# Expert blocks of two 64-row halves with own experts as column tiles, and a second accumulator

## The reference, cut to what matters

```python
def swiglu(x, w_in, w_out):
    g, up = jnp.split(x @ w_in, 2, axis=-1)
    return (jax.nn.silu(g) * up) @ w_out
...
    def body(acc, blk):
        tok, gw, e = blk
        yb = swiglu(xt[tok], w_exp_in[e], w_exp_out[e]) * gw[:, None].astype(xt.dtype)
        return acc.at[tok].add(yb), None
...
    u = ln_plain(x) * (1.0 + scale2) + shift2
    x = ln_affine(DN_ALPHA * x + gate2 * moe(u, p), p['ln2_g'], p['ln2_b'])
```

## Time and profile before

| | |
|---|---|
| median of 3 runs | 2882.27 us (2881.45 to 2883.31) |
| span of the profiled execution | 2881.8 us |
| PE busy | 2738.3 us (95%) |
| DVE / ACT / POOL busy | 1581.8 (55%) / 691.3 (24%) / 1076.2 us (37%) |
| expert loop on PE | 1450.85 us to about 2826 us |
| output stage | from 2829.66 us to the end |

### The profile page before, as it was taken

The page is one execution under the profiler, slowest core; times in us unless marked ns, Lnnn a source line. Parts: engine busy times, 40 slices in busy tenths (PEclk is TensorE's granted clock), DMA queues, the critical chain, the costliest instruction groups (busy, mean ns, idle before and its releaser), DMA issues.

```text
span 2881.8 us, 31407 instructions
## 1 busy us (share of the span) xinstructions
PE 2738.3 (95%) x9145; PEld 1334.1 (46%) x9145; DVE 1581.8 (55%) x2551; ACT 691.3 (24%) x1204; POOL 1076.2 (37%) x1128
## 2 busy tenths in 40 slices
PE   7999999899999999899899999999999999999992
PEld 2345444455555455455444444444444444444440
DVE  4477356778877577778733344334343343333336
ACT  2354354366666311111100000000000000000004
POOL 2002001100000123233456656566565666556654
PEclk9999999899999999999899999999999999999996
DMA  9531010310000311311288798986978688899847
GB/s 350 182 115 55 19 33 8 128 44 12 12 12 8 136 59 59 109 60 59 76 268 233 229 324 228 315 253 166 285 220 264 183 248 248 257 306 287 244 96 255
DMA packets 189138, 464.37 MB, mean 161 GB/s; under 512 B 22524, under 2 KB 47294, under 8 KB 187646
## 3 DMA queue, kind: packets, MB, share of 16 engines
q1 hardware_dynamic: 138142, 311.89, 30.3%
q0 software_dynamic: 50912, 151.41, 21.3%
HBM read 359.28 MB, written 99.75 MB: 159 GB/s over the span
## 4 chain that ended last, share of the span: by engine, by line
PE 58%; DVE 4%; DMA 2%; issue 1%; POOL 1%; ACT 0%; DVEq 0%; SPq 0%; POOLq 0%
PE mx_pH L1263 30%; PE mx_pU L1280 15%; PE mx_pA L1901 3%; PE mx_pL L1901 3%; PE mx_pU L1963 2%; PE mx_pH L1926 2%; PE mx_pB L1934 1%; DMA s_acc<-mx_wso,ex_sidx 1%; PE mx_pB L1250 1%; DVE ring L1397 1%; DMA kT<-s_u,ex_gidx 1%; PE mx_pA L1938 0%; PE mx_pU L1911 0%; DVE mx_st L1723 0%; DMA ring<-s_acc 0%
## 5 line engine op out<-in xcount | busy, mean ns | idle before, releaser
L1263 PE MATMUL mx_pH<-ring,mx_wsi 128*128 (+1 forms) x2080 | 937.2, 593 | 6.4 <-DVE mx_h L1181 3.4
L1096 POOL DMA_INDIRECT kT<-s_u,ex_gidx x516 | 570.4, 1105 | 158.9 <-issue 153.5
L1263 PEld LDWEIGHTS mx_pH<-ring,mx_wsi 128*128 128x128 f32 x2080 | 385.4, 190 | 443.7 <-issue 443.7
L1280 PE MATMUL mx_pU<-qT,mx_hT 128*128 x1040 | 467.6, 592 | 1.5 <-DVE mx_wso L1204 1.5
L1177 DVE STREAM_TRANSPOSE mx_wsi<-kT 128x1024 f32<-128x1024 f32 x130 | 161.6, 1243 | 350.4 <-DMA kT<-s_u,ex_gidx 350.3
L1280 PEld LDWEIGHTS mx_pU<-qT,mx_hT 128*128 128x128 f32 x1040 | 197.5, 190 | 250.0 <-issue 250.0
L1120 POOL DMA_INDIRECT s_acc<-mx_wso,ex_sidx x130 | 212.2, 1632 | 189.5 <-DVE mx_wso L1204 126.7
L1204 DVE SCALAR_TENSOR_TENSOR mx_wso<-mx_pU,mx_wsi 128x1024 f32<-128x1024 f32 x130 | 166.9, 1284 | 186.5 <-PE mx_pU L1280 182.7
L1151 ACT ACTIVATE mx_hT<-mx_pB 128x256 f32<-128x256 f32 x130 | 49.8, 383 | 868.3 <-PE mx_pB L1250 868.3
L639 PE MATMUL fr_pF<-fr_uT,fr_wf 128*128 128x512 f32 x512 | 224.9, 595 | 1.3 <-ACT fr_uT L333 1.3
L1181 DVE TENSOR_TENSOR mx_h<-mx_silu,mx_pH 128x256 f32<-128x256 f32 x130 | 54.1, 416 | 305.9 <-ACT mx_silu L1141 305.6
(11 more groups left out here) (317 smaller groups left out, 3166.6 us busy)
## 6 DMA issues: line engine op xcount, KB each, us to landing
ring<-in_w_exp_in SPq DMA_DIRECT2D x64, 2048.0 KB, 13.8
qT<-in_w_exp_out SPq DMA_DIRECT2D x64, 1024.0 KB, 16.3
fr_wq<-in_w_ada SPq DMA_DIRECT2D x32, 512.0 KB, 4.9
kT<-s_u,ex_gidx POOLq DMA_INDIRECT x520
fr_wf<-in_w_in SPq DMA_DIRECT2D x16, 512.0 KB, 5.7
s_u<-v SPq DMA_DIRECT2D x16, 512.0 KB, 2.6
ring<-s_acc SPq DMA_DIRECT2D x16, 512.0 KB, 13.1
y<-ring SPq DMA_DIRECT2D x16, 512.0 KB, 6.7
```

Source lines behind the costliest of these rows:

```text
L1096: nc.gpsimd.indirect_dma_start(xg[:, u, g, :], None, u2_q, bass.IndirectOffsetOnAxis(ap=gidx[:, u, g:g + 1].bitcast(U32), axis=0)).then_in ...
L1263: m = nc.tensor.matmul(pH[:], xT[:, u, k, :], wi[:, bass.ds(slot, 1), k, :].rearrange("p a f -> p (a f)"), start=(k == 0), stop=(k == KD - 1))
L1280: m = nc.tensor.matmul(pY[:, h, :], hT[:, c, :], wo[:, bass.ds(slot, 1), c, h * 512:(h + 1) * 512].rearrange("p a d -> p (a d)"), start=(c ...
```

## The change

A block keeps its 128 rows, but it is made of two halves of 64 rows (`HALVES`, `ROWS`), each of one expert; neighbouring halves can belong to different experts. An expert has ceil(count / 64) halves, at least one, the first expert at least two. The places of the lists, `s_block` and the running count are in halves; the running count that the weight ring uses is rounded up to blocks.

On PE each matmul of `first`, `second` and `gated` becomes two, with 64 stationary columns each: the lower half goes to PSUM partitions 0 to 63, the upper to 64 to 127 (column tiles). The lower half reads the weights from the ring. The upper half reads them from a place of its own, one copy of an expert's weights, which ACT fills for every block: three copies for the input weights once `first` of the block before is done, one for the output weights once `second` of the block before is done. ACT reads the expert's number with a register load of its own. The transposes of `gated` are now matmuls by the identity.

On SP the loads of input and output weights have semaphores of their own; in each turn SP asks for an input load, waits for the output load of the expert before, asks for the output load, and waits for the input load.

The two halves of a block can hold the same token, so the upper rows are added into a second accumulator, rows T + P on of `s_acc`. It is cleared during the attention by 17 transfers of 512 KB. In `output` each tile has two loads, PE sums both by the identity into one of three PSUM banks, and ACT and DVE read it there; tile 1 is treated as the others.

The diff, cut to its core:

```diff
+HALVES = 2
+ROWS = P // HALVES
...
+                sp.dma_start(acc_d[(t - 1) * P + T:t * P + T, :], acc_d[T:T + P, :]).then_inc(cleared, 16)
...
-                load(r, w_exp_in[bass.ds(q * RING + r, 1)].rearrange("a (k p) f -> p (a k) f", p=P),
-                     w_exp_out[bass.ds(q * RING + r, 1)].rearrange("a (c p) d -> p (a c) d", p=P))
-
-                sp.wait_ge(w_in[(r - 1) % RING], q * 32 + 32)
-                sp.sem_inc(w_ready, 1)
...
+                load_in(r, w_exp_in[bass.ds(q * RING + r, 1)].rearrange("a (k p) f -> p (a k) f", p=P))
+                out_place((r - 1) % RING, q + 1 if r else q)
+                load_out(r, w_exp_out[bass.ds(q * RING + r, 1)].rearrange("a (c p) d -> p (a c) d", p=P))
+                in_place(r, q + 1)
...
+        def first_weights(e):
+
+            act.wait_ge(in_loaded, e + 1)
+            slot = e % RING
+            for k0, k1 in IN_PARTS:
+                nc.scalar.activation(own_in(k0, k1), wi[:, bass.ds(slot, 1), k0:k1, :].rearrange("p a k f -> p (a k f)"), ACT.Copy).then_inc(in_ready, 1)
+
+        def second_weights(e):
+            act.wait_ge(out_loaded, e + 1)
+            nc.scalar.activation(own_out, wo[:, bass.ds(e % RING, 1), :, :].rearrange("p a c d -> p (a c) d"), ACT.Copy).then_inc(out_ready, 1)
...
                 b = t * 2 + u
+                act.reg_mov(there, expert_of(b + 2))
                 gated_rows(b)
                 silu(b + 1)
+                first_weights(kept(there))
+                act.wait_ge(y_mm, b + 2)
+                second_weights(kept(here))
+                act.reg_mov(here, kept(there))
...
             for c in range(FC):
-                m = nc.tensor.transpose(pG[:, c * P:(c + 1) * P], hg[:, c * P:(c + 1) * P], ident)
+                for half in (low, high):
+                    m = nc.tensor.matmul(pG[half, c * P:(c + 1) * P], hg[:, c * P + half.start:c * P + half.stop], ident, start=True, stop=True)
...
+            for p, (k0, k1) in enumerate(IN_PARTS):
+                if k0 == KD // 2:
                     gated(b - 1)
+                pe.wait_ge(in_ready, (b - 1) * len(IN_PARTS) + p + 1)
+                for k in range(k0, k1):
+                    nc.tensor.matmul(pH[low, :], xT[:, u, k, low], wi[:, bass.ds(slot, 1), k, :].rearrange("p a f -> p (a f)"), start=(k == 0), stop=(k == KD - 1))
+                    m = nc.tensor.matmul(pH[high, :], xT[:, u, k, high], own_in(k, k + 1), start=(k == 0), stop=(k == KD - 1))
...
                 for c in range(FC):
-                    m = nc.tensor.matmul(pY[:, h, :], hT[:, c, :], wo[:, bass.ds(slot, 1), c, h * 512:(h + 1) * 512].rearrange("p a d -> p (a d)"),
-                                         start=(c == 0), stop=(c == FC - 1))
+                    nc.tensor.matmul(pY[low, h, :], hT[:, c, low], wo[:, bass.ds(slot, 1), c, cols].rearrange("p a d -> p (a d)"), start=(c == 0), stop=(c == FC - 1))
+                    m = nc.tensor.matmul(pY[high, h, :], hT[:, c, high], own_out[:, c, cols], start=(c == 0), stop=(c == FC - 1))
...
+        sp.wait_ge(scattered, n * 32)
         for t in range(NT):
-            if t == NT - NT // RING:
-
-                sp.wait_ge(h_mm, n * 2 + 1)
             sp.dma_start(z[:, t, :], acc_d[t * P:(t + 1) * P, :]).then_inc(loaded[t], 16)
+            sp.dma_start(z_other[t], acc_d[T + P + t * P:T + P + (t + 1) * P, :]).then_inc(loaded[t], 16)
...
+    def tensor_part(pe):
+        for t in range(NT):
+            pe.wait_ge(loaded[t], 32)
+            if t >= len(banks):
+                pe.wait_ge(centred, t - len(banks) + 1)
+            for h in range(2):
+                half_of = slice(h * 512, (h + 1) * 512)
+                nc.tensor.matmul(banks[t % len(banks)][:, h, :], turn, z[:, t, half_of], start=True, stop=False)
+                m = nc.tensor.matmul(banks[t % len(banks)][:, h, :], turn, z_other[t][:, half_of], start=False, stop=True)
+            m.then_inc(summed, 1)
```

More of the change, by code:

```diff
@@ L729, in front, with attention @@
     nc.all_engine_barrier()
-def attention(nc, hr, mod_d, lru_d, w_out, chan_gain, qx, keep, lruT, shared, apart):
+def attention(nc, hr, mod_d, lru_d, acc_d, w_out, chan_gain, qx, keep, lruT, shared, apart):
     qT, kT, v = keep
@@ L818, in _ @@
                 queries(t)
+                sp.dma_start(acc_d[(t - 1) * P + T:t * P + T, :], acc_d[T:T + P, :]).then_inc(cleared, 16)
+            for t in range(NT, NT + 3):
+                sp.dma_start(acc_d[(t - 1) * P + T:t * P + T, :], acc_d[T:T + P, :]).then_inc(cleared, 16)
+            sp.wait_ge(cleared, 16 * (NT + 1))
         @block.scalar
@@ L1016, in attention, with experts @@
     nc.all_engine_barrier()
-def experts(nc, ctx, u2_d, acc_d, count_d, block_d, left, weights, cst, places_left, banks, signals, apart):
+def experts(nc, ctx, u2_d, acc_d, count_d, block_d, left, weights, cst, places_left, own, banks, signals, apart):
     FH = 2 * D_E
@@ L1031, in experts @@
     pL, pA, pY, pH, pG = banks
-    tables_out, z_stored, z_ready = signals
+    tables_out, z_stored, z_ready, u2_stored = signals
+    own_in, own_out = own
     sem = lambda n: ctx.enter_context(nc.semaphore("ex_" + n))
@@ L1299, in experts, with output @@
     return (sync_part, gpsimd_part, scalar_part, vector_places, vector_part, tensor_part), (pairs, MAXB, scattered, h_mm)
-def output(nc, ctx, acc_d, count_d, ln2_rows, y_d, places_left, added, rows_used, apart):
-    ring, ln, xt, half, small = places_left
+def output(nc, ctx, acc_d, count_d, ln2_rows, y_d, places_left, turn, banks, added, apart):
+    ring, ln, xt, half, small, others = places_left
     pairs, MAXB, scattered, h_mm = added
@@ L1360, in scalar_part @@
         mean(1)
-        for n in range(1, NT - 1):
-            if n + 1 < NT - 1:
-                mean(n + 1)
-            squares(n)
+        for t in range(1, NT):
+            if t + 1 < NT:
+                mean(t + 1)
+            squares(t)
     def vector_part(dve):
-        step = Chain(dve, steps)
-        def own_stats(t):
-            dve.wait_ge(loaded[t], 16)
-            for c in range(2):
-                i = nc.vector.bn_stats(st[:, c, :], z[:, t, c * 512:(c + 1) * 512])
-            step(i)
-            passed(dve, apart)
-            step(nc.vector.bn_aggr(mv, st.rearrange("p a s -> p (a s)")))
-        def variance(t):
-            if t == 1:
-                nc.vector.tensor_scalar(ve[:, t:t + 1], mv[:, 1:2], EPS, None, ALU.add).then_inc(var_ready, 1)
-            else:
-                dve.wait_ge(squared, turns.index(t) + 1)
-                nc.vector.tensor_scalar(ve[:, t:t + 1], sqs[:, t:t + 1], 1.0 / D, EPS, ALU.mult, ALU.add).then_inc(var_ready, 1)
-        own_stats(1)
+        def variance(t):
+            dve.wait_ge(squared, t + 1)
+            nc.vector.tensor_scalar(ve[:, t:t + 1], sqs[:, t:t + 1], 1.0 / D, EPS, ALU.mult, ALU.add).then_inc(var_ready, 1)
         variance(0)
@@ L1812, in tables @@
                 dve.wait_ge(count_mm, 1)
[L1813 to L1819 removed]
+                nblk, cum, done = ez[:, 0, :], sg, ez[:, 1, :]
@@ new lines, in tables, with rounded_up @@
+                part, over_sum, at, over_n = tb[:, 0:2], tb[:, 2:4], tb[:, 4:6], tb[:, 6:8]
+                by_part = lambda x: x.unsqueeze(1).to_broadcast([P, HALVES, N_EXP])
+                by_expert = lambda x: x.unsqueeze(2).to_broadcast([P, HALVES, N_EXP])
+                def rounded_up(out, x, n, least):
+                    step(nc.vector.tensor_scalar(out, x, 1.0 / n, 0.5 - 0.5 / n, ALU.mult, ALU.add))
+                    step(nc.vector.tensor_scalar(out, out, float(2 ** 23), None, ALU.add))
+                    step(nc.vector.tensor_scalar(out, out, -float(2 ** 23), least, ALU.add, ALU.max))
@@ L1836, in tables @@
-                step(nc.vector.tensor_scalar(sm[:, 6:7], cum[:, N_EXP - 1:N_EXP], -3.0, None, ALU.add))
+                for c in range(HALVES):
+                    i = nc.vector.tensor_scalar(part[:, c:c + 1], tok0[:], float(HALVES), float(c), ALU.mult, ALU.add)
+                step(i)
+                over, before = junk[:, 0, 0:HALVES, :], junk[:, 1, 0:HALVES, :]
+                step(nc.vector.tensor_tensor(over, by_part(cum[:]), by_expert(part), ALU.is_le))
+                step(nc.vector.tensor_reduce(over_n, over, AX.X, ALU.add))
@@ new lines, in tables @@
+                step(nc.vector.tensor_tensor(before, over, by_part(nblk), ALU.mult))
+                step(nc.vector.tensor_reduce(over_sum, before, AX.X, ALU.add))
+                step(nc.vector.tensor_tensor(at, part, over_sum, ALU.subtract))
+                step(nc.vector.scalar_tensor_tensor(at, over_n, float(T // ROWS), at, ALU.mult, ALU.add))
+                for c in range(HALVES):
+                    i = nc.vector.tensor_scalar(at[:, c:c + 1], at[:, c:c + 1], float(N_EXP * T // ROWS + c), None, ALU.min)
```

241 lines of the change are left out of this document (124 added, 117 removed).

## The result

The changed kernel takes 3064.45 us (median of 4 runs, 3036.93 to 3076.02), beside 2881.86 for the kernel before: ratio 1.0616, 95% interval 1.0568 to 1.0664. The prediction was 2771 us with a range to 2835, so it has the wrong sign and misses by 293 us.

A forecast was written before the change was run, and what follows sets the result against it. The prediction took PE's matmul records in the expert loop as the bound: -161 (fewer blocks) + 2.5 (last copy) + 18 (late weights) + 34 (end) - 3 (start) = -110 from 2881.8, so 2771 us, range 2745 to 2835.

The forecast's parts named there:

- What a block costs now: Expert loop on PE: 24 pair steps of 0.429 plus 0.44 for transposes, 10.74 us a block, 1203 us for 112.
- The copies on ScalarE: ACT's weight copies and two register loads (1.26 + 0.8 us) per block stay hidden; only the last block adds 2.5 us.
- Fewer blocks: Expert loop: halves of 64 rows make 112 blocks instead of 130; the path before holds 1364 us, gain 161 us.
- pace of the pairs: Expert loop on PE: both column tiles run at once, 0.429 us a pair, with no extra charged per step.
- The rivals on the pace: Each pair pays more: 0.05 extra gives 2905 us, 0.53 a step 3042; loss from 0.470; chance 0.11.
- turns: Rival: the two column tiles on PE take turns, +1153 us, 3924 us; chance 0.02.
- The share for column tiles: Rival from the skill: 79% of ideal for column tiles, an estimated step of 0.54 us; no separate chance.
- Weights arriving late: Expert loop: PE waits for weight loads, 18 us in sum, some 10 us of it near block 30.
- Weights as the bound: Rival: weight loads of 14.3 to 16.3 us, waits of 39 to 86 us, 2792 to 2839 us; chance 0.17.
- The end: Output stage: a ring of engine waits sets 4.4 us a tile, 85.7 us against 52.1, +34 us.
- The rival of a half clock: Output stage: short PE waits keep the clock at 0.50, sums take 6.86 us, 2812 us; chance 0.05.
- The start: Before the expert loop: less index work and less weight traffic beside the second gather, -3 us.

The follow-up runs named there:

- the load moved out of the traffic: Changed kernel with PE's load of the expert number, still from memory, moved from the end of `first` to its middle: 2840.11 us.
- the traffic taken away: Changed kernel, loads from memory, SP moving an eighth of input and half of output weights, POOL scattering 2 of 128 rows: 2761.31 us.
- the version with all tables in SBUF: Changed kernel with PE, ACT and SP reading expert numbers and running count from tables in SBUF instead of memory: 2780.48 us.
- the run with light weights: The version with all tables in SBUF, plus mean and squares tile by tile in the output, SP moving an eighth of input, half of output weights: 2752.43 us.
- after: The changed kernel as profiled, all its register loads from memory: profiled span 3060.7 us, median of runs 3064.45 us.
- PE's loads cured: Changed kernel with only PE reading its expert number from the table in SBUF instead of memory: 2817.59 us.
- With light weights: Changed kernel, all loads from memory, SP moving an eighth of an expert's input weights and half of its output weights: 2830.15 us.
- while POOL adds: The version with all tables in SBUF, mean and squares tile by tile in the output, POOL summing odd tiles and PE even ones: 2761.41 us.

## Why the prediction was wrong

**The step that failed** is "What a block costs now": "Block: 10.30 + 0.44 = 10.74 us, times 112". It adds up matmul records alone and so puts PE's own register loads, which stand between `first` and `second` in every block, at nothing, without a reason; it rests on "what makes fewer PE records saves time one for one", read from the kernel before, where nothing waits for these loads. The line on them was in rows 8. The prediction used it in "The copies on ScalarE" to price ACT's new loads, "just hidden", and never asked whether PE's own stay hidden. Measured, `second` starts 1.92 us later in a block by the mean and then takes 0.68 us longer: 213 and 76 us.

The cover of the loads was the sequencer's lead, 7.07 us, and the change halves exactly that. The two factors multiply: the lead of 18 records is now 3.64 us, and the load moved within the block from 0.02 to 3.67 us, into the traffic of weights and scatter, where it takes 4.8 us by the mean instead of 3.1. An estimate from the two traces parts them, with each load's own length and the 0.7 us behind it: the short lead with the loads of before gives some 63 us of gaps, the long lead with the loads of now some 21, both together 212. Neither was run alone. What was run: 3064 us with both, 2840 with the load moved out of the traffic, 2761 with the traffic taken away (17 us of that are the late weights').

**Its other steps hold**, but for that on ACT, as the version with all tables in SBUF shows, at 2780.5 us against 2771:

- *Fewer blocks, pace of the pairs.* 112 blocks; pairs start 0.429 us apart and a calm block takes 10.74 us (median), as predicted from four records of the attention. A calm block is one in which PE waits for nothing. The rivals on the pace (0.470 and 0.53 us a step) and on turns are refuted. The share for column tiles in the Trainium skill, "TensorE: Matmul & The Clock Gate", Measured speedup vs the span model, by which a step was an estimated 0.54, is not seen here; the rule of the Trainium skill that a change of the tiling mode drains the array while a change of tile does not ("TensorEngine Tiling (Array Packing)", Key Properties) agrees with the trace, where pairs of alternating tiles start 0.429 us apart.
- *Weights arriving late.* Predicted 18 us, with one wait of some 10; measured 17.9 in three waits, the longest 13.5 and at the 30th block as predicted, and 16.7 us of time by the run with light weights. That the sum agrees to 0.1 us is luck: the long wait is 3.5 us longer than predicted, and 4.3 us of it remain with light weights. "Weights as the bound" did not come.
- *The end.* Predicted 85.7 us from the first load to the end, sums 4.4 apart; in after the first load is issued at 2975.66, 85.0 us ahead of the end, and in the version with all tables two sums take 8.66 us, 4.33 each. The rival of a half clock there did not come; it came in the loop.
- *ACT.* The prediction called the loads ahead of `hT` just hidden. They were not: with PE's loads cured, 17 waits for `hT` took 20.7 us, and the loads of ACT and SP together cost 37.
- *The start.* Predicted -3. The `first` that rows 13 show at 1462.73 starts at 1460.32 in after and at 1465.01 in the version with all tables: executions scatter by as much as the term, so it stays open.

**The rivals** of the prediction asked about tiles, weights and the clock, that is, about what the change adds. None asked what the change makes faster on PE and what had been living in that time.

## What to carry to other kernels

When an engine's instructions get shorter, or two run at once, list all that its sequencer does between them (register loads, waits, branches) and hold each against the new lead, not the old one. Registers that a loop needs in every pass should come from a table in SBUF: 0.30 us here, against 2.0 us at best for both parts and 6.0 by the mean where a weight transfer is under way. And a duration read in the trace belongs to its place in the block: if the change moves an access to memory into the traffic of another engine, its price is that of the busy place.

## What the runs showed of the hardware

- PE's sequencer runs ahead of the array by a number of records, not by a time: 17 before, in 7.07 us; 18 in the versions with tiles and a load from memory, in 3.64 us, or 4.1 where the load stands in the middle of `first`. Where the load is from SBUF it starts 0.11 us later, 16 records ahead. "TensorE: Matmul & The Clock Gate" of the Trainium skill, Architectural detail, gives TensorE a queue of 64 instructions; that a queue is counted in instructions agrees, the number seen here is smaller even with the 18 weight loads counted in.
- A register load from memory has two parts. In quiet they take 1.06 and 0.66 us; beside a weight transfer the pointer's takes 4.4 (mean), beside the scatter the value's 2.1. In the Trainium skill, "DMA: Bandwidth & Descriptors", Latency and other measured facts, the floor of such a load is about 0.6 us, which the value's 0.66 confirms, and memory answers in 0.2 us on average and 2 us at high load. The direction agrees; a pointer load of up to 6.1 us is beyond both figures. From SBUF a load takes 0.27 to 0.32 us in the version with all tables there, whatever the traffic.
- Which of the two, the wait in memory or in the path there, makes it long was not told apart. The gathers' data, 512 KB a block as well, has no effect that shows; the scatter's, which is added to what stands in memory, has.
- In the block shown PE came back from 3.27 us without work at a granted clock of 0.53. By the sum over the loop that costs a third of the pauses again, 76 us beside 213, but it is not spread evenly: in 36 blocks `second` ran slower, in the other 74 it did not. From `first` to `second` it was 4.2 us by the mean in the 36, 1.5 in the 74. With light weights, where 100 waits are 0.7 us at most, the granted clock is 1.00.
- VectorE's pass over two SBUF operands takes 2.6 us instead of 1.28 where it starts while POOL adds (2.35 us), and ends 1.1 us after the addition. "SBUF — State Buffer" of the Trainium skill, Terms, says that the two share a pair of ports and that the loser is blocked for the other's whole instruction; the run agrees: a pass of 1.28 us that ends 1.1 us after the addition did nearly all of its work behind it.
